# Where the eight late parts of the modulation are computed in a 1-core transformer kernel: TensorE products against GpSimd products with ScalarE row sums

## The reference, cut to what matters

```python
mod_l = (jax.nn.silu(c) @ w_mod[i] + b_mod[i])[:, None, :]
mod_c = (jax.nn.silu(c_ctx) @ w_mod[i] + b_mod[i])[None, None, :]
sh1_l, sc1_l, g1_l, sh2_l, sc2_l, g2_l = jnp.split(mod_l, 6, axis=-1)
p_l = modulate(rmsnorm(h_lat, norm1[i]), sh1_l, sc1_l) @ w_in[i]
mix_l = jnp.concatenate([o_ssd_l, o_hy_l], axis=-1) @ w_out[i]
h_lat = h_lat + g1_l * mix_l
f_l = modulate(rmsnorm(h_lat, norm2[i]), sh2_l, sc2_l)
h_lat = h_lat + g2_l * peer(f_l, ...)
```

## Time and profile before

| what | us |
|---|---|
| median of 3 runs (lowest, highest) | 4587.32 (4578.32, 4604.14) |
| the profiled execution's own time | 4583.49 |
| its span in the profile | 4581.6 |
| TensorE busy | 4400.6 (96% of the span) |
| VectorE busy | 3165.6 |
| ScalarE busy | 1792.4 |
| GpSimd busy | 1540.8 |
| mean granted TensorE clock, of full speed | 0.972 |

### The profile page before, as it was taken

How to read it: one execution, slowest core, us unless ns; L and a number is a source line. 1 busy time by engine, 2 the same in 40 slices (tenths; PEclk the granted TensorE clock), 3 DMA queues, 4 the chain that set the end, 5 groups by cost and what they waited for, 6 DMA issues and landing times.

```text
span 4581.6 us, 64527 instructions
## 1 busy us (share of the span) xinstructions
PE 4400.6 (96%) x25239; PEld 3816.7 (83%) x25239; DVE 3165.6 (69%) x4827; ACT 1792.4 (39%) x2753; POOL 1540.8 (34%) x977
## 2 busy tenths in 40 slices
PE   7999999999989999999999999899999999999998
PEld 4757855779989999999999876799799878886997
DVE  4756657559868988788788355687388356555873
ACT  4334311233334543333355255354355243223552
POOL 2042024315887657777612100212212101122121
PEclk8999999999999999999999999899999999999999
DMA  4142421224876689999733221132222222001322
GB/s 176 51 146 99 142 68 47 96 87 160 262 244 216 246 320 392 372 386 387 278 102 98 97 75 56 60 111 97 83 97 97 97 80 80 24 18 66 111 98 74
DMA packets 229014, 664.15 MB, mean 145 GB/s; under 512 B 22039, under 2 KB 87975, under 8 KB 226536
## 3 DMA queue, kind: packets, MB, share of 16 engines
q1 hardware_dynamic: 112832, 398.26, 25.6%
q0 software_dynamic: 38752, 143.03, 8.4%
q10 hardware_dynamic: 77128, 118.73, 7.1%
HBM read 591.78 MB, written 68.16 MB: 144 GB/s over the span
## 4 chain that ended last, share of the span: by engine, by line
PE 80%; DVE 13%; POOL 3%; issue 2%; ACT 2%; DMA 1%; DVEq 0%; ACTq 0%; POOLq 0%; SPq 0%
PE ps L258 14%; PE ps L259 14%; PE ps L260 14%; PE ps L2647 6%; PE ps L2649 6%; PE ps L2648 5%; PE ps L1537 2%; DVE r L227 2%; DVE A L1966 2%; PE ps L585 1%; PE ps L1616 1%; DVE A L2265 1%; PE ps L3667 1%; POOL r L227 1%; DMA A<-in_w_mod 1%
## 5 line engine op out<-in xcount | busy, mean ns | idle before, releaser
L258 PE MATMUL ps<-r,r 128*128 128x384 f32 (+2 forms) x3880 | 1427.2, 368 | 19.3 <-POOL r L227 14.2
L259 PE MATMUL ps<-r,r 128*128 128x384 f32 (+2 forms) x3880 | 1410.0, 363 | 0.0
L260 PE MATMUL ps<-r,r 128*128 128x384 f32 (+2 forms) x3880 | 1409.2, 363 | 0.0
L227 DVE TENSOR_TENSOR r<-A,r 128x1024 fp32r<-128x1024 f32 x428 | 582.9, 1362 | 723.1 <-ACT r L221 722.8
L221 ACT ACTIVATE r<-A 128x1024 fp32r<-128x1024 f32 x505 | 534.5, 1059 | 1244.1 <-PE ps L260 1051.7
L258 PEld LDWEIGHTS ps<-r,r 128*128 128x128 f32 x3880 | 732.7, 189 | 110.7 <-issue 21.8
L259 PEld LDWEIGHTS ps<-r,r 128*128 128x128 f32 x3880 | 732.6, 189 | 79.3 <-issue 3.4
L260 PEld LDWEIGHTS ps<-r,r 128*128 128x128 f32 x3880 | 731.9, 189 | 78.8
L274 ACT ACTIVATE r<-A 128x512 fp32r<-128x512 f32 (+1 forms) x824 | 492.3, 611 | 519.4 <-DVE A L2339 237.8
L2647 PE MATMUL ps<-r,r 128*128 128x256 f32 x2240 | 635.9, 284 | 33.2 <-ACT A L2740 30.2
L2649 PE MATMUL ps<-r,r 128*128 128x256 f32 x2240 | 634.8, 283 | 0.0
(11 more groups left out here) (526 smaller groups left out, 5830.8 us busy)
## 6 DMA issues: line engine op xcount, KB each, us to landing
A<-in_pu SPq DMA_DIRECT2D x128, 512.0 KB, 4.4
A<-in_pv SPq DMA_DIRECT2D x128, 512.0 KB, 6.8
A<-in_f1i SPq DMA_DIRECT2D x88, 512.0 KB, 3.5
A<-in_f2i SPq DMA_DIRECT2D x88, 512.0 KB, 3.5
A<-in_w_mod SPq DMA_DIRECT2D x48, 512.0 KB, 4.3
A<-in_w_in SPq DMA_DIRECT2D x48, 512.0 KB, 3.6
acts<-A ACTq DMA_DIRECT2D x128, 192.0 KB, 4.3
gates<-A ACTq DMA_DIRECT2D x8, 3072.0 KB, 11.4
```

The costliest lines, as they stand in the source:

```text
L227: e.tensor_tensor(self.vr(at + 1024, 1024), self.v(self.st0 + 1024 * (u % RS), 1024), self.vr(at, 1024).bitcast(F32), ALU.subtract).then_i ...
L258: t.matmul(o, hi, xh, start=first and k == k0, stop=False)
L259: t.matmul(o, hi, xl, start=False, stop=False)
L260: m = t.matmul(o, lo, xh, start=False, stop=final and k == K - 1)
```

## The change

The stream no longer holds `w_mod` units 16 to 47, so `w_in` follows whole after 16 units. All modulation work is gone from the states and prod stages. The late matrix comes transposed in 64 pieces n of 128x512 (`w_late`, 256 KB each): piece n holds 128 outputs as partitions and one half of the 1024 inputs. `c` comes as a row repeated on 128 partitions. In each of the 32 steps of gate and short, SyncE loads two pieces into two buffers, GpSimd multiplies each by its half of silu(c), and ScalarE sums the two products of the step before by a copy with a row sum. VectorE adds the halves and the bias in the long stage. With `w_mod` gone from states and prod, the last three steps of conv now round the first three gate units, and the step-14 `weights_v` moves behind the "to end weights".

```diff
-    out = [("w_mod", 0, 16), ("w_in", 0, 16), ("w_mod", 16, 32), ("w_in", 16, 32), ("w_out", 0, 16), ("wq", 0, 16),
+    out = [("w_mod", 0, 16), ("w_in", 0, 48), ("w_out", 0, 16), ("wq", 0, 16),
...
+        L.CBC, L.LATE, L.SUMS = 50472, (51496, 52584), 52520
...
         for o in range(16):
-            self.weights_v(v, 8)
+            if o != 14:
+                self.weights_v(v, 8)
...
                 v.tensor_tensor(self.v(L.DW, 192), self.v(L.DTE, 192), self.v(L.DT, 192), ALU.mult).then_inc(*S.on("v", "to end weights"))
+                self.weights_v(v, 8)
...
-            for g in range(3 * n, 3 * n + 3) if n < 8 else ():
-                if g == 16:
-                    t.wait_ge(*S.at("modrow", 4))
-                self.modmm_t(t, 4 + g // 8, 6 + g // 8 % 2, range(g % 8, g % 8 + 1))
-            if n in (5, 7):
-                self.modtr_t(t, (n + 3) // 2, 4 + (n + 3) // 2 % 2)
...
-            if o < 5 and o != 1:
-                t.wait_ge(*S.at("modrow", 6 + o))
-                self.modmm_t(t, 7 + o, 6)
-            if o < 6:
-                if o:
-                    t.wait_ge(*S.at("modset", 5 + o))
-                self.modtr_t(t, 6 + o, 7)
...
+    def late_half(self, n):
+        return self.L1.LATE[n % 2]
+
+    def late_s(self, s, step):
+        S, L = self.S, self.L1
+        if step == 0:
+            for k in range(8):
+                s.wait_ge(*S.at("xn lo", k))
+            s.dma_start(self.v(L.CBC, 1024), self.T["c_row"]).then_inc(*S.dma("crow", "c row"))
+        for n in (2 * step, 2 * step + 1):
+            if n >= 2:
+                s.wait_ge(*S.at("late sum", n - 2))
+            s.dma_start(self.v(self.late_half(n), 512), self.T["w_late"][n]).then_inc(*S.dma(f"late{n % 2}", "late load", n))
+
+    def late_a(self, a, step):
+        S, L = self.S, self.L1
+        if step == 0:
+            a.wait_ge(*S.at("c row"))
+            a.activation(self.v(L.CBC, 1024), self.v(L.CBC, 1024), ACT.Silu).then_inc(*S.on("a", "silu row"))
+            return
+        for n in (2 * step - 2, 2 * step - 1):
+            x = self.v(self.late_half(n), 512)
+            a.wait_ge(*S.at("late product", n))
+            a.activation(x, x, ACT.Copy, accum_out=self.v(L.SUMS + 32 * (n % 2) + n // 2, 1)).then_inc(*S.on("a", "late sum", n))
+
+    def late_g(self, g, step):
...
+        for n in (2 * step, 2 * step + 1):
+            x = self.v(self.late_half(n), 512)
+            g.wait_ge(*S.at("late load", n))
+            g.tensor_tensor(x, x, self.v(L.CBC + 512 * (n % 2), 512), ALU.mult).then_inc(*S.on("g", "late product", n))
...
     def gate_s(self, s):
         S, L = self.S, self.L1
         for o in range(8):
             self.weights_s(s, 8)
+            self.late_s(s, o)
...
                 a.activation(self.v(L.WK + 512 * (o % 2), 512), PS[o % 4][:, :], ACT.Silu).then_inc(*S.on("a", "z", o))
+                self.late_a(a, o)
...
     def short_s(self, s):
         for o in range(24):
             self.weights_s(s, 8)
+            self.late_s(s, o + 8)
...
             a.activation(self.v(L.WK + 514 * (o % 2) + 1, 512), self.PS[o % 3][:, :], ACT.Copy).then_inc(*S.on("a", "short in", o))
+            self.late_a(a, o + 8)
...
+        self.late_a(a, 32)
...
     def short_g(self, g):
         S, L = self.S, self.L2
-        self.after(g, "g", "gate")
         for o in range(24):
             self.weights_g(g, 8)
+            self.late_g(g, o + 8)
+            if o == 8:
+                self.after(g, "g", "gate")
...
+            if r == 0:
+                self.late_v(v)
```

More of the change, by code:

```diff
@@ L950, in states_g @@
         g.wait_ge(*S.at("to end weights"))
-        for n in range(3):
-            self.weights_g(g, 32)
         for n, (d, c) in enumerate(self.WALK):
@@ L987, in states_v @@
         self.after(v, "v", "conv")
-        for n in range(3):
-            self.weights_v(v, 32)
         for n, (d, c) in enumerate(self.WALK):
@@ L1021, in states_a @@
         self.after(a, "a", "conv")
-        for n in range(3):
-            self.weights_a(a, 32)
         for c in (0, 3, 2, 1):
@@ L1030, in states_a @@
         self.end("a", "states")
-    def states_s(self, s):
-        for n in range(3):
-            self.weights_s(s, 32)
     def prod_s(self, s):
         S, L = self.S, self.L1
-        for o in range(2):
-            self.weights_s(s, 32)
         s.wait_ge(*S.at("xn stored"))
         s.wait_ge(*S.at("t", "end", "states"))
[L1044 to L1049, removed]
+        for k in range(8):
             s.dma_start(self.v(L.XR[k], 512), self.xnd[:, 512 * k:512 * k + 512]).then_inc(*S.dma(f"xnr{k}", "xn back", k))
@@ L1173, in prod_v @@
         self.y_v(v, 7)
-        self.modcol_v(v, 2, 32, "norm2")
         for k in (5, 6):
@@ L1201, in prod_g, with late_v @@
             self.gate_lo(g, "g", k)
+    def late_half(self, n):
[3 more added lines that the diff above has]
+        if step == 0:
+            for k in range(8):
+                s.wait_ge(*S.at("xn lo", k))
[15 more added lines that the diff above has]
+    def late_g(self, g, step):
+        S, L = self.S, self.L1
+        if step == 0:
+            g.wait_ge(*S.at("silu row"))
+        for n in (2 * step, 2 * step + 1):
+            x = self.v(self.late_half(n), 512)
+            g.wait_ge(*S.at("late load", n))
+            g.tensor_tensor(x, x, self.v(L.CBC + 512 * (n % 2), 512), ALU.mult).then_inc(*S.on("g", "late product", n))
+    def late_v(self, v):
+        S, L = self.S, self.L1
+        m, one, two = self.v(self.MOD + 16, 32), self.v(L.SUMS, 32), self.v(L.SUMS + 32, 32)
+        v.wait_ge(*S.at("late sum", 63))
+        v.tensor_tensor(m, one, two, ALU.add).then_inc(*S.on("v"))
+        v.wait_ge(*S.last("v"))
+        v.tensor_tensor(m, m, self.prm("b_mod", 16, 32), ALU.add).then_inc(*S.on("v", "late rows"))
+        v.wait_ge(*S.last("v"))
+        self.modcol_v(v, 2, 32, "norm2")
     def gate_s(self, s):
@@ L1291, in gate_g @@
             self.weights_g(g, 8)
+            self.late_g(g, o)
         self.end("g", "gate")
@@ L4248, in sync @@
         self.conv_s(s)
-        self.states_s(s)
         self.prod_s(s)
@@ L4441, in lay_out @@
         "xT": np.ascontiguousarray(I["x"][0].T), "ctxT": np.ascontiguousarray(I["ctx"][0].T),
-        "w_mod": np.ascontiguousarray(I["w_mod"][0].reshape(4, 2, 128, 12, 512).transpose(3, 0, 2, 1, 4)).reshape(48, 128, 1024),
+        "w_mod": np.ascontiguousarray(I["w_mod"][0][:, :2048].reshape(4, 2, 128, 4, 512).transpose(3, 0, 2, 1, 4)).reshape(16, 128, 1024),
+        "w_late": np.ascontiguousarray(I["w_mod"][0][:, 2048:].T.reshape(32, 128, 2, 512).transpose(0, 2, 1, 3)).reshape(64, 128, 512),
+        "c_row": np.ascontiguousarray(row(I["c"])),
         "w_in": blocks(np.concatenate([w_in[:, 1024:3072], w_in[:, :1024], w_in[:, 3104:]], 1)),
```

17 lines of the change are left out of this document (removed).

## The result

The changed kernel takes 4621.03 us (median of 9 runs, 4615.77 to 4640.1), the kernel before 4586.63 us (9 runs, 4577.5 to 4604.14): ratio 1.0079, 95% interval [1.0062, 1.0096]. It is slower by about 34 us. The forecast was 4595 us with "within 0.5%" as its likeliest outcome; what came lies outside that and 6 us above the forecast's own range of 4578 to 4615 us, where the rival "the ring is dearer" was forecast, at 4618 us. The profiled execution took 4617.69 us.

The account below looks back on a forecast made before the run. TensorE was taken to bound most stages, VectorE about as closely in states. Then +49.8 - 39.8 + 0.5 = +10.5 us on the profiled 4583.5 us gave 4594 us, forecast as 4595 us; range 4578 to 4615 us.

Parts of the forecast that it names:

- the ring is dearer: Rival for gate and short: slower unit load and dearer row sums, a turn of 7.9 us, 4618 us; chance 0.13 to 0.18.
- Part 1: End of conv: added rounding work makes VectorE start the states 2.4 us later, at 229.6 us; bounds nothing and 4.6 us.
- Part 2: States: without modulation VectorE binds for 33.5 us, first C by B product at 263.1 us, 8.7 us gained.
- Part 3: Prod without modulation: 105.4 us plus 2 us from first C by B product to H(0), gain 31.2 us.
- H(0): Start of ScalarE's rounding in gate's step 0; forecast 370.5 us, 39.8 us earlier than before.
- Part 4: Gate and short: SyncE's waits for sums delay unit loads, turns of 7.1 us, H(31) at H(0) + 236.2, 49.8 us more.
- the ring: Closed order of waits in gate and short: sums, late loads, unit load, rounding, eviction, sums; 7.1 us a turn.
- The second bulk: Short's 3 MB of transfers, slowing a unit load: 5.5 us, taken as less than the tables.
- H(31): Start of ScalarE's rounding in short's step 23; 596.72 us before the change, forecast near 607 us.
- part 5: Long: three small VectorE operations for the late rows, 0.5 us; the last two sums costed at nothing, 6 us if uncovered.
- The clock's fall: Rival: TensorE's clock falls in gate and short because it waits, about 30 us more, 4625 us; chance 0.07.
- The projections cover the late work: Rival: in gate and short the waits don't bind and the 39.8 us gain stays, 4545 us; chance 0.13.

Follow-up runs that it names:

- Run 1: The changed kernel with SyncE issuing each unit load one step ahead, before its wait for this step's sums: 4556.75 us, ratio 0.9945.
- run 3: The changed kernel with waits, products and sums kept but only the first two of 64 pieces loaded: 4588.02 us, ratio 1.0003.
- run 8: The changed kernel with a third buffer for the late pieces, SyncE's order kept: 4582.74 us, ratio 0.9998.
- run 11: The changed kernel with its own order and two buffers, only the bulk transfers cut into parts: 4611.06 us, ratio 1.0067.
- run 7: The changed kernel with unit loads one step ahead and a third buffer for the late pieces: 4554.19 us, ratio 0.9937.

## Why the prediction was right, and where it was not

- **Part 1 (conv's end, +2.4 us).** VectorE starts the states at 232.97 us instead of 229.6. Of the 5.7 us, 1.9 us are there at conv's first rounding (87.42 against 85.48 us), ahead of anything the change touches. The tail's own part is 3.8 us, within the bounds of 0 and 4.6, near the upper one.
- **Part 2 (states 33.5 us).** Measured 34.8 us from the first copy to 267.8; C by B at 267.84 instead of 263.1 us, which is part 1's 3.4 us and 1.3 us here. The stalls beside GpSimd stayed: the first three that VectorE's decays met lasted 1.77, 2.16 and 1.62 us in place of 0.69 us, and GpSimd's products average 2.06 us.
- **Part 3 (107.4 us).** Measured 107.6 us. So H(0) came at 375.48 instead of 370.5 us, a gain of 34.9 us instead of 39.8; that is just below the 35 to 45 us that I had asked for.
- **Part 4, the mechanism.** Right in each link: roundings released by the load, loads issued behind the sums, H(2) = H(0) + 19.13 us (predicted 19.0), the table loads' 1.3 us in gate's steps 3, 5 and 7. Run 1 shows it by opening the ring.
- **Part 4, the size: the step that failed** is the term "behind a piece of half the size I take 3.85 us". Of the turn's terms, 0.4 us to the issue came out as 0.39 us, and rounding to the end of the sums (my 0.96, 0.5, 0.53, 0.63 and twice 0.1, so 2.82 us) as 2.77 us. The landing was 4.70 us in the median instead of 3.85 us. That makes 7.86 us instead of 7.1 us, and 22 us in 29 turns. There were two pieces ahead of the unit, and I had counted one; runs 3 and 8 show 3.55 us behind none, 3.70 us behind one. The second of a pair in the earlier trace rows had 4.4 us, and that was the nearest row, as the same 512 KB stood in front; with it the turn would have been 7.6 us. The turn's range was too narrow as well: the bounds of its terms add up to 6.4 and 7.8 us and not to 6.6 and 7.7, and 7.86 us lies above both.
- **The second bulk.** 5.5 us taken; the turn of 16.31 us is 8.4 us over a plain one, with a load of 13.1 us: 2.9 us short. I had it cheaper than the tables "since they are issued just behind a unit load"; here they were issued from 484.5 us on and the unit's load at 487.4 us, behind them. The tables' turn took H(2) to H(0) + 19.13 us as forecast. Together: 29 times 7.86, 3.8 and 8.4 us are 240.1 us, and the trace has 240.7 us from H(2) to H(31). The 2 us for stores have no place in this sum.
- **The sum.** At H(31) the forecast was H(0) + 236.2 us, so 606.7 us; it came at 635.28 us, 28.6 us later: 5.0 us by H(0) and 23.6 us in the stretch. At the end it is 23.8 us (34.3 us late where 10.5 were forecast), as 4.3 us came back behind H(31), and I had 0.5 us for part 5. There is a slip at the sum's end too: 4594 us is the profiled execution, and the 3.8 us to the median would have made it 4598 us and not 4595.
- **Part 5** held: nothing waits visibly for the last sums.
- **The rivals.** The dearer ring had its cause half right: the unit's load as slow as the second of a pair and more (4.70 against its 4.4 us), but the row sum at 0.1 us and not 0.2. That its turn of 7.9 us met 7.86 us is partly luck, as the two errors cancel. The clock's fall was seen too (0.94 against 1.00), but TensorE doesn't bind here: only 8.8 us of the roundings' waits end with TensorE, and with the ring open (run 1) the granted clock is 0.99 from 404 to 560 us. VectorE wasn't held up to the point of binding. "The projections cover the late work" is false for this order of issue and nearly true for run 1's.
- **The bulk transfers' price.** The unit load beside the tables took 10.36 us here, as the row of before had it (10.8 us). The forecast's other reading, that a load which takes turns with the tables waits little longer than its own data, is wrong for a reason that the trace of before shows. From 418 to 424 us the tables' queue (q10) and the unit loads' queue (q1) moved (packets, MB, share of the DMA engines):

```profile
q10 hardware_dynamic: 142, 2.06, 80.4%
q1 hardware_dynamic: 141, 0.51, 20.9%
```

  The turns are even in packets, but the tables' packets are four times as large, so the unit load gets a fifth of the bytes. It also starts late: issued at 412.7 us, it had no packet before 416.4 us, while a load issued at 543.1 us with the queues quiet had its first within 1.3 us; what holds it back isn't shown. The Trainium skill's rule ("DMA: Bandwidth & Descriptors", section "Queues, rings and completion order"), that each DMA engine serves its queue rows in turn, packet by packet, agrees with these counts; it says nothing of equal bytes, and it was read so. Cut into 512 KB parts, the tables held the next load up little: in run 11 the rounding behind the first part waited 5.14 us for its unit, as in a plain turn.

## What to carry to other kernels

Before a wait is put into a queue that also carries a prefetch, write down what stands behind it: a load that was issued three units ahead is worth nothing once it stands behind a wait on this step's own work, and no busy time shows it. Sum the closed path (issue, landing, use, release) and compare it with the bounding engine's step; if it is longer, put the prefetch ahead of the wait, and count in its landing all the bytes that the same queue issues in front of it. Beside a bulk transfer on another queue, compare the sizes of the packets: what is shared evenly is their number. Here that one call is worth 63 us of a stretch of 260 us, and turns a loss of 0.8% into a gain of 0.6%.

## What the runs showed of the hardware that I had not expected

- A sum by `accum_out` (the turn at 588 us above) shows as a second instruction, ACTIVATION_READ_ACCUMULATOR, of 190 ns; in pitch it adds 0.10 us (sum to sum 0.62 us, activation to its read 0.52 us).
- The cost of transfers in front of a 512 KB load isn't even: one 256 KB piece ahead cost 0.15 us, the second 1.0 us (3.55, 3.70, 4.70 us).
- A 512 KB load beside 3 MB from ScalarE's queue took 13.1 us, longer than beside the 4 MB of tables (10.4 us); the 3 MB hold a store of 2 MB. What of it is the store was tried in parts only (run 11).
- Two queues with work took turns packet for packet, 142 against 141, but with 2.06 MB against 0.51 MB, as their packets differ in size.
- Runs 7 and 8, on one chip and with nothing different up to there, reached conv's first rounding 3.7 us apart (84.05 and 87.73 us), which is more than several of the differences looked for here.
